# Score blocks of the dilated heads issued two query tiles at a time

## Chip, cores and metric

The kernel runs on one core of one Trainium2 chip. The metric is device time of one execution in microseconds (us). Where the text says TensorE, VectorE, ScalarE and GpSimd, the profile's rows say PE (PEld for its weight loads), DVE, ACT and POOL.

## What is computed

A two-layer encoder trunk on x of 1 x 1024 x 1024 (float32). Layer 0: RMS norm, one projection to queries, keys and values of 16 heads of width 64, of which eight are dilated sliding-window heads (mixer A) and eight 2-D neighbourhood heads; output projection, residual, SwiGLU feed-forward, residual. Layer 1: the same with eight differential heads. A last RMS norm. The change touches mixer A alone:

```
DILATED_PAIRS = ((128, 1), (512, 4), (2048, 16))

def dilated_window_branch(q, k, v, slopes, window, dilation):
    # query t attends to t + j*dilation, |j| <= window/(2*dilation)
    s = einsum(q, k) * HEAD_DIM ** -0.5 - slopes * dist
    s = where(valid, s, -inf)
    m = max(s); p = exp(s - m); l = sum(p)
    return einsum(p, v) / l, m + log(l)

def dilated_mixture_attention(q, k, v):
    # the three branches, weighted by softmax over their log denominators
```

## The kernel before

Everything is float32, and products are kept exact to float32 by splitting an operand into a high and a low part and adding two or three matmuls. Sizes: 1024 tokens are NQ = 8 query tiles of 128; two heads of a mixer make a head pair P. P = 0 to 3 are the dilated pairs (kind A), 4 to 7 the neighbourhood pairs (B), 8 to 15 the differential heads (C).

The order of every engine is written out by hand. `order(0)` runs through (P, n), head pair and query tile, and each engine has a loop body for that *turn*; engines meet at semaphores only. On TensorE (`attention_mixed`, line 2346) a turn of kind A holds:

- `qk(*after)`, line 2185: the scores of the **next** tile. For each head of the pair (m = 0, 1) three near matmuls (lines 2203 to 2209, 128 queries by 256 neighbouring keys) and three far ones (line 2213, queries and keys taken with a stride of four). They contract over 64 rows; the two heads lie on rows 0 to 63 and 64 to 127. Scores go to PSUM banks 2 (n % 2) + m, so tile n + 2 uses the banks of tile n, and `qk` waits until the exponentials of tile n have read them (`exp_done`). In turn 7 the block (tile 0 of the next pair) stands between the two transposes (`late_scores`).
- in even turns `pv`, lines 2274 and 2278: the product of the last two tiles' weights with the values, head 0 before `turn(.., 0)` and head 1 before `turn(.., 1)`.
- `turn`, line 2244: transposes of the exponentials of tile n, head 0 and head 1. They wait for `exp_done` and, since the transposed bank is used again, for the low part of the tile before (`lo_done`).
- `fill`, line 2147: matmuls of the projection for the next pair, in pieces given by the tables FILLS_AB (P < 3) and FILLS_TURN (P = 3). 24 of them make one 128 x 512 piece in the single fill bank 7; the first of a piece waits for `fill_evac`.
- `tv`, line 2160: transposes of the next pair's values, waiting for `vlo_done` and `fill_evac`; and in turn 1 of P = 1 to 5 `turn_stats`, lines 2169 and 2173, transposes of softmax statistics that wait for `y_done` and, from P = 2, for `al_done`.

VectorE in a turn: `evac` (lines 1491, 1493, 1496) of a finished fill piece, `ttr` (line 1525, bias and minimum of the next tile's scores, after `qk_done`), `y_add` (line 1613) of the output pieces, `lo` (line 1606, low part of the transposed exponentials), `vlo` (line 1509), `w_split` (line 1383). In turn 0 of P = 1 and 2 the evac stands near the turn's end, behind `y_add` (and from P = 2 behind `weights_last`, lines 1547 and 1551). In turn 4 of P < 3 the last `lo` is put off to turn 5 (`lower_later`), behind the evac. ScalarE: `y_copy` (line 994), `hi` (line 948), `exp` (line 913, two for each head, waiting for `ttr_done` and for the transposes of the tile before, because there is one exponential tile for each head), `kq_high` (line 928), `vhi` (line 941).

Of the kernel before, what the change touches and what calls it, by code (L numbers as in the profile page):

```python
# [25 lines left out]
NQ = T // 128  # L26
# [33 lines left out]
def key_tiles(kind, n):  # L60

    if kind != "B":
        return 0, NQ
    lo = max(0, min(2 * n - ROWS // 2, 2 * NQ - ROWS))
    hi = max(0, min(2 * n + 1 - ROWS // 2, 2 * NQ - ROWS)) + ROWS
    return lo // 2, (hi + 1) // 2 - lo // 2
# [14 lines left out]
def build(nc, x_in, wstrips, wdown, gains, subln, lams, ali_a, ali_c, tab_b, out):  # L81
# [141 lines left out]
    def kind_of(P):  # L223
        return "A" if P < 4 else "B" if P < 8 else "C"
# [162 lines left out]
    def fills_at(P, n):  # L387

        parts = FILLS_AB[n] if P < 3 else FILLS_TURN[n] if P == 3 else FILLS_B[n] if P < 8 else FILLS_LATE[n]
        if P == 2 and n == NQ - 1:  # L390
            return [parts[0], [(2, 2, 0, 8)]]
        if P == 8 and n == 0:
            return [[(0, 1, 7, 14)], [(0, 1, 14, 24)]]
        known = [(0, late(P)), (1, P % 8 < 7), (2, P < 2)]
        return [[p for p in part if (p[0], True) in known] for part in parts]
# [34 lines left out]
    def turned_v(P, n):  # L430

        if P == 0 and n < 2:
            return ([(0, 0), (0, 1)], [(0, 2), (0, 3)]) if n == 0 else ([(0, 4), (1, 0)], [(1, 1)])
        if 3 <= P < 8:
            return [(P, 1)] if late(P) and n == 1 else [], [(P + 1, 0)] if P < 7 and n == 7 else []
        if late(P):
            first, second = {0: ([], [0]), 1: ([1], [])}.get(n, ([], []))
            return [(P, b) for b in first], [(P, b) for b in second]
        first, second = {1: ([0], [1]), 3: ([2], [3]), 5: ([4], [])}.get(n, ([], []))
        return [(P + 1, b) for b in first], [(P + 1, b) for b in second]  # L440
# [20 lines left out]
    def order(layer):  # L461

        for g in range(8 * NQ):
            P, n = 8 * layer + g // NQ, g % NQ
            after = (8 * layer + (g + 1) // NQ, (g + 1) % NQ) if g + 1 < 8 * NQ else None
            last = (P, n - 1) if n else (P - 1, NQ - 1)
            yield P, n, after, last if g and n % 2 == 0 else None, P % 8 < 7
# [1596 lines left out]
    def pe_program(e):  # L2064
# [120 lines left out]
        def qk(P, n):  # L2185

            kind = kind_of(P)
            k0, nk = key_tiles(kind, n)
            if kind == "A":
                e.wait_ge(S["kq_lo"], 4 * P + (3 if n == 0 else 4))  # L2190
                if 8 * P + n > 1:
                    e.wait_ge(S["exp_done"], 1 + 2 * (8 * P + n - 1))
                if P == 0 and n == 0:
                    e.wait_ge(S["fill_evac"], 4)
                t = 128 * n - BAND
                near = slice(128 * n, 128 * n + 128)
                far = slice(n // 2 + 512 * (n % 2), 512 * (n % 2) + 512, NCLS)
                for i, (a, b) in enumerate(((0, 0), (0, 1), (1, 0))):
                    for m in range(2):
                        r = slice(64 * m, 64 * m + 64)  # L2200
                        ps, q, k = PS[:, 2 * (n % 2) + m, :], QS[r, a, near], KS[r, P % 2, b, :]
                        if 0 < n < NQ - 1:
                            e.matmul(ps[:, 0:256], q, k[:, t:t + 256], start=i == 0, stop=False)  # L2203
                        elif n == 0:
                            e.matmul(ps[:, 0:BAND], q, k[:, 0:BAND], start=i == 0, stop=False)
                            e.matmul(ps[:, BAND:256], q, k[:, 0:256 - BAND], start=False, stop=False)
                        else:
                            e.matmul(ps[:, 0:256 - BAND], q, k[:, t:T], start=i == 0, stop=False)
                            e.matmul(ps[:, 256 - BAND:256], q, k[:, T - BAND:T], start=False, stop=False)
                for i, (a, b) in enumerate(((0, 0), (0, 1), (1, 0))):  # L2210
                    for m in range(2):
                        r = slice(64 * m, 64 * m + 64)
                        last = e.matmul(PS[:, 2 * (n % 2) + m, 256:512], QS[r, a, far],  # L2213
                                        KS[r, P % 2, b, n // 2:T:NCLS], start=False, stop=i == 2)
                last.then_inc(S["qk_done"], 1)
                return
            e.wait_ge(S["kq_lo"], 4 * P + (3 if n < 4 else 4))
            e.wait_ge(S["exp_done"], 1 + 16 * P + 2 * n)
            if P == 8 and n == 0:
                e.wait_ge(S["fill_evac"], 6 * P + 3)  # L2220
            q = slice(128 * n, 128 * n + 128)
            for c in range(0, nk, 4):
                wd = 128 * min(4, nk - c)
                k = slice(128 * (k0 + c), 128 * (k0 + c) + wd)
                for i, (a, b) in enumerate(((0, 0), (0, 1), (1, 0))):
                    for m in range(2):
                        r = slice(64 * m, 64 * m + 64)
                        last = e.matmul(PS[:, S_BANK[m] + c // 4, 0:wd], QS[r, a, q], KS[r, P % 2, b, k],  # L2228
                                        start=i == 0, stop=i == 2)
            last.then_inc(S["qk_done"], 1)  # L2230
# [111 lines left out]
        def fills(parts, P, layer):  # L2342
            for ahead, k, a, b in parts:
                fill(P + ahead, k, a, b, layer)

        def attention_mixed():
            begin(0)
            for P, n, after, last, more in order(0):
                kind = kind_of(P)
                first_part, second_part = fills_at(P, n)  # L2350
                first, second = turned_v(P, n)
                late_scores = kind == "A" and n == NQ - 1
                late_turn = kind == "B" and n == NQ - 1 and P < 7
                if after and not late_scores:
                    qk(*after)
                if P == 0 and n == 1:
                    tv(*first.pop(0), P, n)
                if late_turn:
                    fills(first_part, P, 0)
                if last:  # L2360
                    if n == 2 and 1 <= P <= 5:
                        e.wait_ge(S["st_copy"], P)
                    if n == 4 and P >= 6:
                        e.wait_ge(S["rows_copied"], P - 5)
                    e.wait_ge(S["vlo_done"], issued(P, n))
                    pv(*last, 0)
                turn(P, n, 0, kind)
                if P == 0 and n == 0:
                    fill(1, 0, 0, 5, 0)
                    tv(0, 0, P, n)  # L2370
                    fill(1, 0, 5, 11, 0)
                    tv(0, 1, P, n)
                    turn(P, n, 1, kind)
                    fill(1, 0, 11, 16, 0)
                    tv(0, 2, P, n)
                    fill(1, 0, 16, 22, 0)
                    tv(0, 3, P, n)
                    fill(1, 0, 22, 24, 0)
                    continue
                if n == 1 and 1 <= P <= 5:  # L2380
                    turn_stats(P)
                if n == 3 and P >= 6:
                    turn_rows(P)
                if not late_turn:
                    fills(first_part, P, 0)
                if late_scores:
                    qk(*after)
                for v in first:
                    tv(*v, P, n)
                if last:  # L2390
                    pv(*last, 1)
                if not after:
                    op_item(0, 0)
                turn(P, n, 1, kind)
                if P < 3:
                    fills(BETWEEN_AB.get(n, []), P, 0)
                for v in second:
                    tv(*v, P, n)
                fills(second_part, P, 0)
            for m in range(2):  # L2400
                op_item(0, m + 1)
                pv(7, NQ - 1, m)
            op_item(0, 3)
            e.wait_ge(S["rwide_done"], 1)
            for n in range(NQ):
                last = e.matmul(PS[:, T_BANK + n // 4, 128 * (n % 4):128 * (n % 4) + 128],
                                BIAS0[:, 0, 128 * n:128 * n + 128], IDENT[:, :], start=True, stop=True)
            last.then_inc(S["lspread_done"], 1)
# [331 lines left out]
```

## Time and profile before

| | us |
|---|---|
| median of 3 runs | 2653.29 |
| lowest and highest | 2650.76, 2653.81 |
| the profiled execution, own time | 2651.4 |
| its span, first to last instruction | 2649.6 |
| mean granted clock of TensorE | 0.991 |
| first and last far score matmul of the dilated pairs, start | 45.4, 286.2 |

The profiled execution's time is its span and 1.8 us around it. Timeline rows give the start in us from the span's start, the time from start to end of a merged group, engine, line, operation and operands. Ends of matmuls are modelled and overlap the next one's start, so the text works with starts.

### The profile page before, as it was taken

The numbers are of one execution on the slowest core, as the hardware profiler recorded it, in microseconds if no ns is written. First come the engines' busy times: TensorE is split into PE (matmuls) and PEld (weight loads), VectorE is DVE, ScalarE is ACT, GpSimd is POOL, SyncE is SP. The second block draws the span as 40 slices with busy tenths as digits, with TensorE's granted clock in tenths as the row PEclk, the third lists the DMA queues.
The fourth block names the chain that finished last, engine by engine and source line by source line (L and its number), as shares of the span: only waits on it lengthen the run. The fifth ranks groups of instructions, "written<-read, shape, count | busy, mean of one in ns | idle before, by whom it ended". The sixth has DMA issues, their size and how long they took to land.

```text
span 2649.6 us, 37390 instructions
## 1 busy us (share of the span) xinstructions
PE 2616.7 (99%) x13531; PEld 2161.0 (82%) x13531; DVE 1774.7 (67%) x2918; ACT 1116.4 (42%) x1998; POOL 141.9 (5%) x142
## 2 busy tenths in 40 slices
PE   8999999899999999999999999999999999999998
PEld 6888878788888888888878888888888888888887
DVE  6566655655676666766777777777656677666766
ACT  5555645534323323333455555555343223323333
POOL 0001022400000000000000000000000000000001
PEclk9999999999999999999999999999999999999999
DMA  3123243521111111111311111111211111111112
GB/s 124 59 59 83 67 120 104 158 104 52 56 48 48 56 59 52 48 52 58 116 46 47 48 48 47 48 48 66 96 56 56 52 48 48 55 58 53 48 48 84
DMA packets 101725, 173.75 MB, mean 66 GB/s; under 512 B 27296, under 2 KB 36944, under 8 KB 100048
## 3 DMA queue, kind: packets, MB, share of 16 engines
q1 hardware_dynamic: 90560, 162.26, 19.4%
q10 hardware_dynamic: 11024, 9.60, 1.3%
q8 instruction: 90, 1.47, 0.2%
q14 instruction: 51, 0.42, 0.0%
HBM read 151.74 MB, written 20.08 MB: 65 GB/s over the span
## 4 chain that ended last, share of the span: by engine, by line
PE 93%; DVE 2%; ACT 2%; issue 1%; SPq 1%; DMA 1%; POOL 0%; ACTq 0%; POOLq 0%; DVEq 0%
PE PS L2147 19%; PE PS L2067 18%; PE PS L2069 18%; PE PS L2068 18%; PE PS L2228 5%; PE PS L2297 5%; PE PS L2253 4%; PE PS L2244 1%; PE PS L2213 1%; PE PS L2274 1%; PE PS L2160 1%; PE PS L2278 1%; SPq L516 0%; PE PS L2203 0%; PE PS L2074 0%
## 5 line engine op out<-in xcount | busy, mean ns | idle before, releaser
L2147 PE MATMUL PS<-HH,WS 128*128 128x512 f32 x1536 | 518.1, 404 | 9.3 <-DVE HL L1405 8.1
L1182 ACT ACTIVATE WS<-WR 128x512 fp32r<-128x512 f32 x254 | 159.3, 629 | 432.3 <-PE PS L2069 310.3
L2147 PEld LDWEIGHTS PS<-HH,WS 128*128 128x128 f32 x1536 | 286.6, 189 | 66.8 <-DVE WS L1411 7.2
L2147 PE MATMUL PS<-HL,WS 128*128 128x512 f32 x768 | 302.8, 394 | 0.0
L2067 PE MATMUL PS<-AH,WS 128*128 128x512 f32 x704 | 275.5, 391 | 0.0
L2069 PE MATMUL PS<-AH,WS 128*128 128x512 f32 x704 | 274.7, 390 | 0.0
L2068 PE MATMUL PS<-AL,WS 128*128 128x512 f32 x704 | 274.6, 390 | 0.0
L1863 DVE TENSOR_TENSOR X<-PS,X 128x512 f32<-128x512 f32 x352 | 231.2, 686 | 63.1 <-PE PS L2069 62.9
L2067 PE MATMUL PS<-TH,WS 128*128 128x512 f32 x640 | 249.0, 389 | 0.0
L2068 PE MATMUL PS<-TL,WS 128*128 128x512 f32 x640 | 249.0, 389 | 0.0
L2069 PE MATMUL PS<-TH,WS 128*128 128x512 f32 x640 | 249.0, 389 | 0.0
L1805 DVE TENSOR_TENSOR WS<-WR,WS 128x512 fp32r<-128x512 f32 x254 | 174.9, 689 | 108.5 <-ACT WS L1182 105.0
L2067 PE MATMUL PS<-FH,WS 128*128 128x512 f32 x608 | 237.2, 390 | 0.5 <-DVE SIL L1857 0.5
L2069 PE MATMUL PS<-FH,WS 128*128 128x512 f32 x608 | 236.6, 389 | 0.0
L2068 PE MATMUL PS<-FL,WS 128*128 128x512 f32 x608 | 236.5, 389 | 0.0
L1531 DVE CUSTOM_DVE_ANT_0 PS<-PS,BIASC 128x1024 f32<-128x1024 f32 x128 | 154.3, 1247 | 26.3 <-PE PS L2228 25.2
L2147 PEld LDWEIGHTS PS<-HL,WS 128*128 128x128 f32 x768 | 145.8, 190 | 25.8
L2069 PEld LDWEIGHTS PS<-AH,WS 128*128 128x128 f32 x704 | 132.5, 188 | 27.7
L2067 PEld LDWEIGHTS PS<-AH,WS 128*128 128x128 f32 x704 | 132.6, 188 | 27.2
L2068 PEld LDWEIGHTS PS<-AL,WS 128*128 128x128 f32 x704 | 132.5, 188 | 27.3
L2228 PE MATMUL PS<-KS,QS 64*128 64x512 f32 (+1 forms) x1056 | 145.7, 406 | 1.5 <-ACT EC L918 0.9
L918 ACT ACTIVATE EC<-PS,ST 128x1024 f32<-128x1024 f32 x128 | 141.2, 1114 | 3.5 <-DVE ST L1531 3.5
(251 smaller groups left out, 4575.8 us busy)
## 6 DMA issues: line engine op xcount, KB each, us to landing
WR<-wstrips SPq DMA_DIRECT2D x304, 256.0 KB, 2.7
DR<-wdown SPq DMA_DIRECT2D x88, 256.0 KB, 2.6
BIASC<-ali_c SPq DMA_DIRECT2D x8, 960.0 KB, 6.9
BIAS<-tab_b SPq DMA_DIRECT2D x4, 1536.0 KB, 9.8
Y<-y_scratch SPq DMA_DIRECT2D x12, 512.0 KB, 8.1
BIAS<-ali_a SPq DMA_DIRECT2D x4, 1152.0 KB, 8.0
ya_scratch<-YS ACTq DMA_DIRECT2D x32, 128.0 KB, 2.4
MA<-a_scratch SPq DMA_DIRECT2D x16, 256.0 KB, 4.8
```

The lines of the kernel that those rows point to most:

```text
L918: e.activation(e_tile(kind, m, n, P)[:, 0:128 * nk], banks(S_BANK[m], 2)[:, 0:128 * nk], ACT.Exp, scale=-1.0, bias=ST[:, n % 2, m:m + 1], ...
L1182: e.activation(WS[:, slot, 0, :], src, ACT.Copy).then_inc(S["w_hi"], 1)
L1531: e.tensor_tensor_reduce(out=s, in0=s, in1=(table if kind == "C" else table[:, m, :])[:, c:c + 128 * nk], scale=-1.0 if kind == "B" else 1 ...
L1805: e.tensor_tensor(WS[:, slot, 1, :], src, f(WS[:, slot, 0, :]), ALU.subtract).then_inc(S["w_lo"], 1)
L1863: e.tensor_tensor(xs, PS[:, D_BANK + at % 4, :], xs, ALU.add).then_inc(S["d_free"], 1)
L2067: e.matmul(ps, wh, xh, start=start, stop=False, skip_group_check=on)
L2068: e.matmul(ps, wh, xl, start=False, stop=False, skip_group_check=on)
L2069: return e.matmul(ps, wl, xh, start=False, stop=stop, skip_group_check=on)
L2147: last = e.matmul(ps, wt, xt, start=g == 0, stop=g == 23)
L2228: last = e.matmul(PS[:, S_BANK[m] + c // 4, 0:wd], QS[r, a, q], KS[r, P % 2, b, k], start=i == 0, stop=i == 2)
L2253: last = e.transpose(PS[:, bank + k // 4, 128 * (k % 4):128 * (k % 4) + 128], src[:, 128 * k:128 * k + 128], IDENT[:, :])
L2297: last = e.matmul(PS[:, bank, lo_:hi_], v, p, start=i == 0, stop=i == len(todo) - 1)
```

## The change

Kind A alone is touched. In turns 0, 2 and 4 of a pair TensorE issues two score blocks, those of tiles n + 1 and n + 2, in turn 6 one (tile 7), and in turns 1, 3 and 5 none. Turn 7 is as before. The other engines' programs are the same, instruction for instruction.

```diff
@@ -2351,7 +2351,10 @@
                 first, second = turned_v(P, n)
                 late_scores = kind == "A" and n == NQ - 1
                 late_turn = kind == "B" and n == NQ - 1 and P < 7
-                if after and not late_scores:
+                if kind == "A" and not late_scores:
+                    for ahead in range(n + 1, min(n + 3, NQ)) if n % 2 == 0 else []:
+                        qk(P, ahead)
+                elif after and not late_scores:
                     qk(*after)
                 if P == 0 and n == 1:
                     tv(*first.pop(0), P, n)
```

TensorE at the head of turn 0 of P = 1: what stands there in the changed kernel against before (lines 2203 and 2213 are a score block, 2274 the start of PV).

```order
 L2203 MATMUL PS<-KS,QS 128x256 x5
 L2213 MATMUL PS<-KS,QS 128x256 x6
+L2203 MATMUL PS<-KS,QS 128x256 [waits exp_done,kq_lo]
+L2203 MATMUL PS<-KS,QS 128x256 x5
+L2213 MATMUL PS<-KS,QS 128x256 x6
 L2274 MATMUL PS<-ATA,VS 128x256 [waits y_done,lo_done,vlo_done]
 L2274 MATMUL PS<-ATA,VS 128x256
```

The scores of tile 2 now stand directly behind those of tile 1, ahead of PV and of everything else in the turn.

TensorE from the end of turn 0 to the first fills of turn 1 of P = 1, before (line 2147 is a fill, 2244 the transposes of exponentials, 2169 the transpose of statistics):

```order
L2147 MATMUL PS<-HH,WS 128x512
L2203 MATMUL PS<-KS,QS 128x256 [waits exp_done,kq_lo]
L2203 MATMUL PS<-KS,QS 128x256 x5
L2213 MATMUL PS<-KS,QS 128x256 x6
L2244 MATMUL PS<-IDENT,E_75 128x128 [waits lo_done,exp_done]
L2244 MATMUL PS<-IDENT,E_75 128x128 x3
L2169 MATMUL PS<-IDENT,SM 32x128 [waits vlo_done,y_done,exp_done]
L2147 MATMUL PS<-HH,WS 128x512 [waits fill_evac]
```

and in the changed kernel:

```order
L2147 MATMUL PS<-HH,WS 128x512
L2244 MATMUL PS<-IDENT,E_75 128x128 [waits lo_done,exp_done]
L2244 MATMUL PS<-IDENT,E_75 128x128 x3
L2169 MATMUL PS<-IDENT,SM 32x128 [waits vlo_done,y_done,exp_done]
L2147 MATMUL PS<-HH,WS 128x512 [waits fill_evac]
```

Between the last fill of turn 0 and the fill that waits for `fill_evac`, the twelve score matmuls are gone.

## Rows read from the trace of the kernel before

**Rows 1.** The page's parts 1 and 2: busy times, and TensorE's granted clock.
```profile
PE 2616.7 (99%) x13531; PEld 2161.0 (82%) x13531; DVE 1774.7 (67%) x2918; ACT 1116.4 (42%) x1998; POOL 141.9 (5%) x142
...
PEclk9999999999999999999999999999999999999999
```

**Rows 2.** The page's part 4, chain that ended last, by engine.
```profile
PE 93%; DVE 2%; ACT 2%; issue 1%; SPq 1%; DMA 1%; POOL 0%; ACTq 0%; POOLq 0%; DVEq 0%
```

**Rows 3.** Timeline, PE, P=1, turns 2 and 3 (several narrow windows): start, length, instruction.
```profile
141.15 0.60 PE L2244 MATMUL PS<-IDENT,E 128*128 128x128 f32 x4
141.50 0.47 PE L2147 MATMUL PS<-HL,WS 128*128 128x512 f32 x1
...
142.97 0.40 PE L2147 MATMUL PS<-HL,WS 128*128 128x512 f32 x1
...
143.64 0.28 PE L2203 MATMUL PS<-KS,QS 64*128 64x256 f32 x2
143.75 0.73 PE L2213 MATMUL PS<-KS,QS 64*128 64x256 f32 x4
...
144.07 0.65 PE L2213 MATMUL PS<-KS,QS 64*128 64x256 f32 x4
...
144.30 0.42 PE L2213 MATMUL PS<-KS,QS 64*128 64x256 f32 x2
...
145.06 0.48 PE L2147 MATMUL PS<-HH,WS 128*128 128x512 f32 x1
```

**Rows 4.** Timeline, P=1, end of turn 0 and turn 1: ACT, DVE, PE.
```profile
125.03 0.47 ACT L913 ACTIVATE E<-PS,SM 128x256 f32<-128x256 f32 x1 [1.58 <-PE PS L2244]
...
126.07 0.59 ACT L994 ACTIVATE YS<-PS 64x512 f32<-64x512 f32 x1
...
127.44 0.67 DVE L1493 TENSOR_TENSOR FS<-PS,RSTD 128x512 f32<-128x512 f32 x1
...
128.35 0.48 PE L2147 MATMUL PS<-HH,WS 128*128 128x512 f32 x1
```

**Rows 5.** Timeline, P=1, turn 5: DVE, PE.
```profile
160.29 0.67 DVE L1493 TENSOR_TENSOR FS<-PS,RSTD 128x512 f32<-128x512 f32 x1
...
161.22 0.48 PE L2147 MATMUL PS<-HH,WS 128*128 128x512 f32 x1
```

**Rows 6.** Timeline, P=1, turn 3: DVE, PE.
```profile
146.26 0.69 DVE L1606 TENSOR_TENSOR ATA<-PS,ATA 128x512 fp32r<-128x512 f32 x1
147.64 0.69 DVE L1493 TENSOR_TENSOR FS<-PS,RSTD 128x512 f32<-128x512 f32 x1 [0.70 <-PE PS L2147]
...
148.39 0.50 PE L2147 MATMUL PS<-HH,WS 128*128 128x512 f32 x1
```

**Rows 7.** Timeline, P=0, turn 1: DVE, PE.
```profile
61.07 0.69 DVE L1509 TENSOR_TENSOR VC<-PS,VC 128x512 fp32r<-128x512 f32 x1 [1.53 <-ACT VC L941]
...
62.15 0.33 PE L2160 MATMUL PS<-IDENT,FS 128*128 128x128 f32 x1
```

**Rows 8.** Timeline, P=3, turns 1, 2 and 4: DVE, ACT, PE.
```profile
256.27 0.19 DVE L1551 TENSOR_TENSOR CA<-CE,CW 128x32 f32<-128x32 f32 x1
...
256.52 0.28 PE L2173 MATMUL PS<-IDENT,CA 128*32 128x128 f32 x1
...
259.49 0.96 PE L2213 MATMUL PS<-KS,QS 64*128 64x256 f32 x6
...
260.29 0.21 ACT L913 ACTIVATION_READ_ACCUMULATOR E<-PS,SM 128x1 f32 x1
...
273.59 0.21 ACT L913 ACTIVATION_READ_ACCUMULATOR E<-PS,SM 128x1 f32 x1
...
273.24 0.87 PE L2274 MATMUL PS<-ATA,VS 128*128 128x256 f32 x6
...
276.75 0.39 PE L2147 MATMUL PS<-HH,WS 128*128 128x512 f32 x1
277.24 0.47 PE L2274 MATMUL PS<-ATA,VS 128*128 128x256 f32 x2
```

## The prediction, made before the changed kernel was run

> **What bounds the kernel now.** I read the busy shares first. TensorE (PE) is busy for 99% of the span, the granted clock is the upper level of 2.4 GHz (a 9 in every slice of its row), and VectorE and ScalarE have a third and more to spare [rows 1]. The chain that ended last is PE for 93% of its length [rows 2]. So the time is the length of PE's own queue plus the places where that queue stands still, and a change that only reorders PE must be judged on two things: how much shorter the queue becomes, and which results are no longer ready when PE comes for them. The third view is the timeline of single PE instructions around a score block, and the fourth the timelines of ScalarE (ACT) and VectorE (DVE) over the same microseconds.
>
> A *turn* is one pass of the loop, one query tile n of one head pair P. A *score block* is one call of qk: six near and six far matmuls on 64 rows.
>
> **What a score block costs alone, and behind another.** Around the block at the head of turn 3 of P=1 [rows 3], the last fill matmul starts at 142.97 and the first fill behind the block and the transposes at 145.06, 2.09 us. Without a block it would be one fill (six of them run from 141.50 to 142.97, 0.24 each) and four transposes (141.15 to 141.50, 0.35), 0.59. The block therefore costs 2.09 - 0.59 = 1.50 us. Inside it the pace is quicker: the last near pair takes 143.75 - 143.64 = 0.11, the first far pair 0.32, the second 0.23. A block with another 64-row block on both sides would be 3 x 0.11 + 0.32 + 2 x 0.23 = 1.11 to 1.13; I take 1.13. The other 0.37 is paid at the change from 128-row to 64-row matmuls and back. The trace has no two blocks in a row, so the saving of a pairing is bounded from above by that 0.37 and from below by nothing at all (the switch could be paid again at the semaphore wait between the two); I take 0.37, because inside a block near and far matmuls follow each other with no such pause. With 12 pairings (tiles 1+2, 3+4, 5+6 of four head pairs) PE's queue becomes 12 x 0.37 = 4.4 us shorter.
> The Trainium skill (TensorEngine Tiling (Array Packing), Key Properties) states that changing the tiling mode drains TensorE while moving between tiles of one mode doesn't; by that rule alone the change would be worth those 4.4 us, and the trace agrees as far as the 0.37 above goes. The same page of the Trainium skill (PSUM Bottleneck) warns that tiling quickens TensorE but not the emptying of PSUM; it gives no price, and speaks the other way.
>
> **What the moved block was covering.** At an odd turn the block stood between the last fills of the even turn and the first work of the odd one. Remove it and PE arrives 1.50 us earlier, relative to everything that ACT and DVE still have to finish from the even turn. Those chains start from PE instructions (last transposes, last PV) that are themselves 1.13 us later, since the extra block stands ahead of them. So a pairing costs 1.13 minus the smaller of 1.50 and the slack at the first wait of the odd turn. With slack above 1.50 it would be -0.37; with no slack it is +1.13. I take the slack from the rows, with 0.06 us from the end of a DVE instruction to the start of the waiting matmul (147.64 + 0.69 = 148.33 to 148.39 in [rows 6]).
>
> *Turn 1, P=1* [rows 4]. Behind the even turn's last transposes ACT runs two exponentials (from 125.03), the copy for the output (126.07), DVE the addition and then evac, whose last instruction ends at 127.44 + 0.67 = 128.11; only then may the fill start that re-uses the fill bank. It starts at 128.35, could at 128.17: slack 0.18, cost 1.13 - 0.18 = +0.95. P=2 is taken as the same; there DVE has two more small instructions in front of that evac, so it is between 0.95 and 1.13.
> *Turn 5, P=1* [rows 5]. The evac that frees the fill bank ends at 160.29 + 0.67 = 160.96; the fill starts at 161.22. Slack 0.20, cost +0.93, three times (P=0, 1, 2).
> *Turn 3, P=1* [rows 6]. Here the evac waits for fills that PE itself brings forward, but DVE has to finish a low part at 146.26 + 0.69 = 146.95 first, so evac ends at 147.64 and the fill can start at 147.70 instead of 148.39. Slack 0.69, cost +0.44, three times.
> *Turn 1, P=0* [rows 7]. PE's first work is the transpose of V that waits for DVE's low part, ended at 61.07 + 0.69 = 61.76. It starts at 62.15, could at 61.82. Slack 0.33, cost +0.80.
> That is 0.80 + 2 x 0.95 + 3 x 0.93 + 3 x 0.44 = 6.8 us for P=0 to 2.
>
> *P=3* has fewer fills per turn and is tighter [rows 8]. Turn 1: the transposes of statistics wait for a DVE result that ends at 256.27 + 0.19 = 256.46 and start at 256.52: slack nil, +1.13. Turn 2: the second block (tile 4) overwrites the banks of tile 2 and must wait for its exponentials, which end at 260.29 + 0.21 = 260.50; PE would be there at 259.49 + 0.78 = 260.27. So 0.29 of waiting and the 1.13, +1.42. What turn 3 would give back, turn 4 takes: its second block (tile 6) waits for the exponentials of tile 4, ended at 273.59 + 0.21 = 273.80 behind DVE's own queue. From 273.86 the block takes 1.13, so the first PV starts at 274.99, not 273.24: +1.75, of which the wait in front of the second PV (276.75 + 0.23 to 277.24, 0.26) takes 0.26 back: +1.49. (The way back to 128 rows, up to 0.1, is left out.) Turns 5 and 6 run behind ACT and DVE and give nothing. P=3 costs 1.13 + 1.42 + 1.49 = 4.0 us.
>
> **Sum.** 6.8 + 4.0 = +10.8 us against the profiled execution's own 2651.4, that is 2662.2. The median of the runs shown lies 1.9 above that execution (2653.3), so the forecast is 2664.1. DVE, ACT and the DMA queues issue the same instructions in the same order; in odd turns DVE finds its scores ready earlier, which costs nothing and gains only where DVE waits for scores and someone waits for DVE. Nothing behind turn 7 of P=3 changes but by the shift. About 0.2% (5.3 us) is what a measurement here can tell from no change.
>
> **Rivals.**
> *The odd turns keep their cover (faster).* If ACT and DVE end the even turn's chains at least 1.5 us sooner, because the early scores empty their queues, every pairing is worth -0.37: 2653.3 - 4.4 = 2648.9. This is what the mode-switch rule of the Trainium skill (TensorEngine Tiling (Array Packing), Key Properties) would give with nothing else in play. It decides where the slack is above 1.13, the point at which a pairing turns from loss to gain. Against it: the chain of turn 1 starts at the even turn's last transposes and has no idle time for scores in it [rows 4].
> *The second block drains too.* If the wait between the two blocks costs the pause again, each pairing loses 0.37 more: 10.8 + 4.4 = +15.2, 2668.5. For it: no two blocks stand together in the trace. Against it: the smooth pace inside a block [rows 3].
> *Half the loss.* In turns 3 and 5 and in P=3 a DVE queue stands ahead of the result; if scores that are there early pull half of it forward, some +5.4 remain, 2658.7.
> *No change that can be measured*: the losses meet waits that exist already. The only ones seen are parts of a microsecond in P=3.
>
> **How the numbers follow.** Forecast 0.70, second drain 0.10, half the loss 0.10, gain 0.04, no change 0.06. Half the loss lies on the border, so it is shared: faster 0.04, the same 0.10, slower 0.86. The forecast itself may be off by 0.1 us at each of twelve waits and by 2 us in P=3, which gives 2660 to 2668; taking in most of the two neighbours the range is 2657.5 to 2669.5.
>
> **What would show it.** In the changed profile: the second block's first near pair follows the last far pair by some 0.23 us; the idle time of PE in front of the fills at odd turns 1 and 5 (released by evac, line 1493) grows to over 1 us each and to 0.8 us in turn 3; a wait for exponentials appears in front of the second blocks of P=3; the stretch from the first to the last turn of the four dilated pairs is 10 to 12 us longer and everything behind it as long as before. A stretch that is shorter, or odd turns without idle time, would show the slack argument wrong.

## The result, and the profile after

| | before | changed |
|---|---|---|
| median of 6 runs, us | 2651.32 | 2665.32 |
| lowest and highest | 2647.81, 2653.81 | 2664.05, 2666.84 |
| the profiled execution, own time | 2651.4 | 2664.05 |
| its span | 2649.6 | 2662.3 |

The ratio is 1.0053, with a 95% interval of 1.0043 to 1.0064: slower by 14.0 us in the medians, by 12.7 us in the two profiled executions. The forecast was 2664.1 and slower, on a median of before of 2653.3; with six runs that median is 2.0 us lower.

The page of the changed kernel, parts 1 and 4:

```profile
PE 2616.6 (98%) x13531; PEld 2162.6 (81%) x13531; DVE 1777.7 (67%) x2918; ACT 1116.2 (42%) x1998; POOL 141.8 (5%) x142
...
PE 90%; DVE 4%; ACT 2%; issue 1%; SPq 1%; DMA 1%; ACTq 0%; POOL 0%; POOLq 0%; DVEq 0%
```

PE is busy for the same 2616.6 us as before (2616.7, [rows 1]); what has grown is the time in which it stands still, and the chain that ended last runs three points less over PE and two more over DVE [rows 2]. Who ends PE's idle time in the dilated stretch, from the view of waits of the changed kernel (engine, instruction, who ended it: us in total, times, longest):

```profile
PEld PS L2147 <- DVE FS L1493: 8.4, 9, 1.3
...
PE PS L2147 <- DVE FS L1493: 6.4, 9, 1.1
...
PE PS L2169 <- issue: 2.7, 3, 1.7
...
PE PS L2203 <- ACT E L913: 1.6, 2, 1.4
PE PS L2244 <- DVE ATA L1606: 1.4, 2, 0.7
PE PS L2160 <- DVE VC L1509: 1.0, 1, 1.0
```

and in the same stretch of the kernel before:

```profile
PEld PS L2147 <- DVE FS L1493: 0.8, 1, 0.8
...
PE PS L2147 <- DVE FS L1493: 0.6, 1, 0.6
```

Nine fills now wait for an evacuation where one did. These are turns 1, 3 and 5 of P = 0 to 2; the one in turn 1 of P=0 was there before. Line 2169, the transpose of statistics in turn 1 of P = 1 to 3, waits too: the view names no releaser, but in P=1 it starts at 130.23, 0.10 behind the end of VectorE's addition (the first row of DVE below), whose semaphore it waits for. The timeline of PE at the first two kinds of place that the prediction spoke of, the pair of blocks in turn 0 of P=1 (a row from a narrow window first) and the start of turn 1:

```profile
121.09 0.42 PE L2213 MATMUL PS<-KS,QS 64*128 64x256 f32 x2
121.33 0.54 PE L2203 MATMUL PS<-KS,QS 64*128 64x256 f32 x6
121.70 0.97 PE L2213 MATMUL PS<-KS,QS 64*128 64x256 f32 x6
...
129.13 0.60 PE L2244 MATMUL PS<-IDENT,E 128*128 128x128 f32 x4
130.23 0.27 PE L2169 MATMUL PS<-IDENT,SM 128*32 128x128 f32 x1 [0.50 <-issue]
130.91 0.50 PE L2147 MATMUL PS<-HH,WS 128*128 128x512 f32 x1 [0.41 <-DVE FS L1493]
```

and DVE over the same time:

```profile
129.45 0.68 DVE L1613 TENSOR_TENSOR YS<-PS,YS 64x512 f32<-64x512 f32 x1 [3.44 <-ACT YS L994]
130.06 0.20 DVE L1491 TENSOR_TENSOR FS<-PS,RSTD 128x64 f32<-128x64 f32 x1
130.19 0.67 DVE L1493 TENSOR_TENSOR FS<-PS,RSTD 128x512 f32<-128x512 f32 x1
```

The second block follows the first after 0.24 us, the pace of far pairs, and its near part takes 0.37 instead of 0.45. Then, 9 us later, the evacuation ends at 130.86 and the fill starts at 130.91, 0.05 behind it. In [rows 4] the fill was 0.24 behind. The transposes at 129.13 were early and the fill had to wait all the same.

**Where the 12.7 us are.** I compare the starts of the transposes of head 1 in both traces, turn by turn, both counted from the first score block. The difference grows by 1.15 in every even turn of P = 0 to 2 that has a pair, and the odd turns give part of it back. (In turn 3 the fill that waits stands behind these transposes. They come 1.5 us sooner, and the wait takes 0.7 of it back before turn 4; the table counts it with turns 2 and 3.)

| pairing | forecast | measured |
|---|---|---|
| P=0, turns 0 and 1 | +0.80 | 1.15 - 0.26 = +0.89 |
| P=1, turns 0 and 1 | +0.95 | 1.15 - 0.16 = +0.99 |
| P=2, turns 0 and 1 | +0.95 | 1.15 - 0.01 = +1.14 |
| P=0 to 2, turns 2 and 3, each | +0.44 | +0.33 |
| P=0 to 2, turns 4 and 5, each | +0.93 | +0.98 |
| sum, P=0 to 2 | +6.8 | +7.0 |
| P=3, turns 0 and 1 | +1.13 | +1.13 |
| P=3, the rest | +2.9 | +5.0 |
| dilated stretch | +10.8 | +13.1 |

The other 0.4 us lie outside the stretch, where both kernels issue the same: the changed trace reaches its first score block 0.6 us sooner, and behind the stretch the difference wanders between 10.9 and 14.3 us and ends at 13.3. TensorE's clock falls there in both kernels, not in the same places: its mean is 0.87 from 510 to 550 us in the trace before and 0.91 from 523.4 to 563.4 in the changed one. A second trace of the changed kernel (below) has the same 13.1 in the stretch and ends at 10.9, so what lies outside the stretch differs by 2 us between executions.

**P=3.** The excess lies in turn 4. PE of the changed kernel there:

```profile
280.67 0.96 PE L2213 MATMUL PS<-KS,QS 64*128 64x256 f32 x6
283.06 0.62 PE L2203 MATMUL PS<-KS,QS 64*128 64x256 f32 x6 [1.42 <-ACT E L913]
283.49 0.99 PE L2213 MATMUL PS<-KS,QS 64*128 64x256 f32 x6
284.40 1.15 PE L2274 MATMUL PS<-ATA,VS 128*128 128x256 f32 x6
285.35 1.16 PE L2278 MATMUL PS<-ATA,VC 128*128 128x256 f32 x4
286.31 1.06 PE L2244 MATMUL PS<-IDENT,E 128*128 128x128 f32 x4
```

The wait for the exponentials of tile 4 is the one forecast. But PV, up to the transposes behind it, takes 1.91 us from 284.40 to 286.31, where before it took 1.24, from 273.24 [rows 8] to this row:

```profile
274.48 0.60 PE L2244 MATMUL PS<-IDENT,E 128*128 128x128 f32 x4
```

The view of windows (stretch, its length, busy us of each engine, granted clock, DMA share, GB/s) tells why:

```profile
281.00:284.40 3.40, 1.98 (x18) 1.49 (x16) 2.82 (x10) 2.92 (x10) 0.41 (x1) 1.00 0.40 142
284.40:288.50 4.10, 4.10 (x20) 3.86 (x19) 2.41 (x10) 1.69 (x5) 0.87 (x1) 0.58 0.00 0
288.50:292.00 3.50, 3.50 (x24) 3.13 (x23) 0.22 (x1) 0.78 (x3) 0.00 (x0) 1.00 0.00 0
```

The granted clock was 1.00 up to 284.4, 0.58 on average in the next 4.1 us, so for most of them the lower level of 1.2 GHz, and 1.00 again. In the 3.4 us ahead of it PE had been busy for 1.98.

### The profile page after: what moved, and what is told of

Same layout as the page of the kernel before. It is cut to its first block, busy times and chain, and to the rows that moved or that the text cites. A ratio compares the mean times of both kernels' runs of the same rounds, so it can differ in the third digit from the quotient of the medians.

```text
span 2662.3 us, 37390 instructions
## 1 busy us (share of the span) xinstructions
PE 2616.6 (98%) x13531; PEld 2162.6 (81%) x13531; DVE 1777.7 (67%) x2918; ACT 1116.2 (42%) x1998; POOL 141.8 (5%) x142
## 4 chain that ended last, share of the span: by engine, by line
PE 90%; DVE 4%; ACT 2%; issue 1%; SPq 1%; DMA 1%; ACTq 0%; POOL 0%; POOLq 0%; DVEq 0%
PE PS L2147 18%; PE PS L2067 18%; PE PS L2068 18%; PE PS L2069 18%; PE PS L2228 5%; PE PS L2297 4%; PE PS L2253 3%; PE PS L2213 1%; PE PS L2274 1%; PE PS L2244 1%; PE PS L2160 1%; PE PS L2278 1%; PE PS L2074 1%; SPq L516 1%; ACT E L913 0%
```

## The experiments

Positions are read as above: the shift of the transposes of head 1 against the kernel before, from the first score block on. "To P=3" is that shift at the end of turn 7 of P=2, "P=3" what its turns add. The pairing as changed gives +7.0 and +6.1.

**Pairings in P = 0 to 2 alone.**

```diff
-                if kind == "A" and not late_scores:
+                if kind == "A" and P < 3 and not late_scores:
```

> The pairing is done for head pairs P = 0 to 2 alone. Theory (each moved block had covered a chain on ScalarE and VectorE; a pairing costs 1.15 us of insertion less the slack at the odd turn): the dilated stretch grows by the 7.0 us that the changed kernel shows up to the first turn of P = 3, so +7 us, near 2658, and the granted clock stays at its upper level in the whole dilated stretch. Rival (the loss comes from the second block's wait for exponentials, which only P = 3 has): within 1 us of before or faster by 9 x 0.37 = 3.3 us.

Measured: ratio 1.0025 (1.0015 to 1.0036), 2658.7 against 2651.4, +7.3. To P=3 the shift is 8.3, of which 1.3 come at once in turn 1 of P=0. The clock had fallen there, against the expectation:

```profile
63.00:70.00 7.00, 5.52 (x23) 4.41 (x24) 3.84 (x13) 2.32 (x8) 0.00 (x0) 0.76 0.00 0
```

All other turns of P = 0 to 2 repeat the changed kernel's steps to 0.04 us, and P=3 adds 0.0. The rival falls: the nine pairings without any wait for exponentials lose by themselves.

**Pairings in P = 3 alone.**

```diff
-                if kind == "A" and not late_scores:
+                if P == 3 and not late_scores:
```

> The pairing is done for P = 3 alone. Theory: +6.1 us, the share that the changed kernel shows between the first turn of P = 3 and its end: 1.1 at turns 0 and 1, 5.0 at turns 2 to 6. Of the 5.0 some 1.7 is the half clock of 3.4 us behind the wait in turn 4, which should come again, since the wait is the same 1.4 us long. If the half clock needs the idle time gathered over P = 0 to 2, it is missing here and the growth is 4.4. Rival (pairing saves the mode switch and P = 3 is not special): -1.1 us.

Measured: 1.0023 (1.0013 to 1.0034), +5.9 in the medians. The shift in P=3 of the profiled execution is +4.5: 1.15, 1.62 and 1.74 for the three pairings. The granted clock is 1.00 over the whole stretch, behind the same wait in turn 4:

```profile
44.00:305.00 261.00, 254.76 (x1626) 210.41 (x1625) 153.38 (x437) 149.19 (x419) 22.81 (x26) 1.00 0.23 61
```

PE there, with the wait:

```profile
276.98 0.62 PE L2203 MATMUL PS<-KS,QS 64*128 64x256 f32 x6 [1.42 <-ACT E L913]
277.42 0.99 PE L2213 MATMUL PS<-KS,QS 64*128 64x256 f32 x6
278.33 0.90 PE L2274 MATMUL PS<-ATA,VS 128*128 128x256 f32 x6
```

So the changed kernel's 6.1 are 4.5 of insertion and waits and 1.6 of half clock, and in this execution the wait in turn 4 alone didn't bring the half clock. It is one execution, and the fastest of the eight (2655.19; the others are 2655.8 to 2661.7). The median's +5.9 is near the 6.1 that was expected with the fall, so the executions that were not profiled may well have had one; no trace shows them.

**The two blocks apart in the same turn.** The second block stands behind the transposes of head 0.

```diff
                 turn(P, n, 0, kind)
+                if kind == "A" and n in (0, 2, 4):
+                    qk(P, n + 2)
```

with `qk(P, n + 1)` alone at the head of even turns.

> As the changed kernel, but in turns 0, 2 and 4 the second score block stands behind the transposes of head 0 instead of directly behind the first block. Theory: the blocks no longer share a mode switch, so each of the nine even turns of P = 0 to 2 grows by 1.50 instead of 1.15, while the odd turns wait as before: +3.2 us over the changed kernel up to the first turn of P = 3. In P = 3 the wait for exponentials shrinks, because PE has work in front of it. If two adjacent blocks save nothing, the stretch up to P = 3 is the same as in the changed kernel.

Measured: 1.0051 (1.0036 to 1.0066). Each even turn of P = 0 to 2 grows by 1.55 instead of 1.15, the odd turns give back what they did, and to P=3 the shift is +10.7, 3.7 more than in the changed kernel. The second block alone, in turn 0 of P=1:

```profile
124.55 0.60 PE L2244 MATMUL PS<-IDENT,E 128*128 128x128 f32 x4
125.08 0.62 PE L2203 MATMUL PS<-KS,QS 64*128 64x256 f32 x6
...
126.43 0.50 PE L2147 MATMUL PS<-HL,WS 128*128 128x512 f32 x1
```

From the transposes to the first fill behind them it is 1.88 us, without a block 0.35 (141.15 to 141.50 in [rows 3]): alone the block costs some 1.5 us, behind another 1.15. That is the saving of a shared mode switch: by the shifts 0.40 us a pairing, forecast 0.37. P=3 adds only 4.3, with no wait for exponentials and a clock of 1.00 throughout, so in the traces the whole stretch is 1.9 us longer than the changed kernel's. The medians are alike (2665.4 and 2665.3); no run shows what makes up for these 1.9 us.

**The evacuation ahead of the addition.** Changed kernel, VectorE's turn 4 of P < 3 (and the evacuation taken out of turn 5):

```diff
+                if n == 4 and P < 3:
+                    evac(P + 1, 3)
                 if last:
                     y_add(*last, 1)
```

> As the changed kernel, but VectorE does the evacuation of the key piece that opens turn 5 of P = 0 to 2 (piece 3 of the next pair) ahead of the last output addition of turn 4, instead of behind it. Theory: the fill at the head of turn 5 waits for exactly that evacuation, behind the addition; without the addition in front it comes 0.6 us sooner, in each of three turns: the wait there falls from 1.3 to about 0.7 us, 1.8 us in all, and the first turn of P = 3 comes 1.8 us earlier than in the changed kernel. Rival (the wait ends with something else, such as transposes or ScalarE): no change.

Measured: 1.0041 (1.0025 to 1.0056), 2661.5, and 2.1 us less shift to P=3 than in the changed kernel: 0.70, 0.71 and 0.74 in turn 5 of P = 0, 1 and 2, nothing anywhere else. Turn 5 of P=1, DVE and PE (PE's lines are two higher here):

```profile
164.07 0.69 DVE L1493 TENSOR_TENSOR FS<-PS,RSTD 128x512 f32<-128x512 f32 x1 [3.32 <-PE PS L2149]
164.68 0.67 DVE L1613 TENSOR_TENSOR YS<-PS,YS 64x512 f32<-64x512 f32 x1
```

```profile
163.88 0.60 PE L2246 MATMUL PS<-IDENT,E 128*128 128x128 f32 x4
164.82 0.50 PE L2149 MATMUL PS<-HH,WS 128*128 128x512 f32 x1 [0.35 <-DVE FS L1493]
```

In the changed kernel the transposes were at 163.42, the evacuation at 164.35 to 165.02 and the fill at 165.08, with 1.05 us of idle time. The two traces have shifted against each other by then, so count from the transposes: the fill starts 0.94 us behind them here and 1.66 there. The wait ends with this evacuation and with nothing else.

**The same move in the kernel before.**

> The kernel before, with the evacuation that opens turn 5 of P = 0 to 2 moved ahead of the last output addition of turn 4. Theory: there the score block covers the chain and 0.2 us of slack are left, so the 0.7 us that the same move gave in the changed kernel are worth nothing: the first turn of P = 3 comes within 0.1 us of before. Rival (a sooner evacuation always helps): 2 us earlier.

Measured: 0.9998 (0.9988 to 1.0007); shift to P=3 0.0. What is worth 2.1 us in the one kernel is worth nothing in the other: there the score block still covers the chain.

**Work put into the hole.** Changed kernel, in turn 1 of P = 1 and 2 and turn 5 of P = 0 to 2, ahead of the transposes of head 0 and behind the waits that these have:

```diff
+                if (n == 1 and P in (1, 2)) or (n == 5 and P < 3):
+                    e.wait_ge(S["exp_done"], 1 + 16 * P + 2 * n + 1)
+                    e.wait_ge(S["lo_done"], 1 + t_count(P, n, 0, kind) - 2)
+                    for again in range(3):
+                        for i, k in enumerate((2, 0, 3, 1)):
+                            e.transpose(PS[:, T_BANK, 128 * i:128 * i + 128],
+                                        e_tile(kind, 0, n)[:, 128 * k:128 * k + 128], IDENT[:, :])
```

> As the changed kernel, but in turn 1 of P = 1 and 2 and turn 5 of P = 0 to 2 TensorE repeats the four transposes of head 0 three times before it does them (the same values into the same place), some 1.1 us of work in each of five places, 5.3 us in all, where the score block stood before. Theory: PE has 1.3 us of idle time there, in which that work disappears; the fill that waits for the evacuation starts when it did, and the first turn of P = 3 comes as in the changed kernel, within 0.3 us. Rival (PE's queue is what counts, there is no chain with a fixed end): 5.3 us later.

Measured: 1.0048 (1.0033 to 1.0064), 2665.3. The shift to P=3 is the changed kernel's to 0.02 us, though each place has 1.3 us more of PE work, some 6.5 us in all. Turn 1 of P=1:

```profile
130.63 1.47 PE L2375 MATMUL PS<-IDENT,E 128*128 128x128 f32 x12
131.94 0.60 PE L2244 MATMUL PS<-IDENT,E 128*128 128x128 f32 x4
132.37 0.27 PE L2169 MATMUL PS<-IDENT,SM 128*32 128x128 f32 x1
132.41 0.50 PE L2147 MATMUL PS<-HH,WS 128*128 128x512 f32 x1
```

DVE's evacuation ends at 131.68 + 0.67 = 132.35. The fill starts 0.06 behind it, as without the extra work. The removed score block had been free of charge at these places for the same reason, but for the 0.2 us of slack. (In P=3 this run has 1.0 us more, with a granted clock of 0.72 from 264 to 270; from 284 to 290 it is 0.74, the fall in turn 4 that the changed kernel has too.) The waits in turn 3 and in turn 1 of P=0 were not tested in this way; for them there are the traces alone.

**Pairs in odd turns.** Turn 0 forms tile 1, turns 1, 3 and 5 form two tiles, turns 2, 4 and 6 none.

```diff
-                    for ahead in range(n + 1, min(n + 3, NQ)) if n % 2 == 0 else []:
+                    for ahead in [1] if n == 0 else [n + 1, n + 2] if n % 2 else []:
```

> The pairing turned round: turn 0 forms tile 1 alone, turns 1, 3 and 5 form tiles 2 and 3, 4 and 5, 6 and 7, turns 2, 4 and 6 none. The same count of mode switches is saved. Theory (1.15 less the slack at the next turn): from the timeline of before for P = 1, turn 2 has 1.30 us of slack at the fill behind its evacuation, turn 4 has 0.3 at the first PV (values' low part ended 152.44, PV at 152.82), turn 6 has more than the block's 1.6: net -0.15, +0.85 and -0.37 to -0.45, so about +0.3 for a pair and +1 up to the first turn of P = 3; P = 3 itself between 0 and +4. In all 2652 to 2656, well under the changed kernel. Rival (any moved block costs about a microsecond): as the changed kernel.

Measured: 1.0018 (1.0009 to 1.0027), 2657.3, clock 1.00 throughout the stretch. It is better than the changed kernel by 8 us and worse than before, as expected in direction, but the size was off: +4.7 to P=3 instead of +1. The pairing at turns 3 and 4 cost 0.97 (expected 0.85), but the one at turns 1 and 2 cost 0.39 (expected -0.15) and the one at 5 and 6 0.26 (expected about -0.4). I had looked at the first wait of each turn. A second one stands further in: the second PV of turn 2 waits for the addition that frees its bank, which VectorE does behind the next tile's scores. PE and DVE of P=1, turn 2:

```profile
141.98 0.68 DVE L1613 TENSOR_TENSOR YS<-PS,YS 64x512 f32<-64x512 f32 x1
...
142.81 0.65 PE L2274 MATMUL PS<-ATA,VS 128*128 128x256 f32 x4 [0.28 <-DVE YS L1613]
```

Turn 6 has the same wait (0.29 of idle time in P=1). Turn 5 also grows by 1.49 instead of 1.15, since its second block is tile 7, at the edge, whose near part is twelve matmuls (lines 2208 and 2209) instead of six. P=3 adds 1.5 us, inside the 0 to 4 that were expected.

**Without the last pairing of P = 3.** As the changed kernel, with tile 6 formed in turn 5.

> As the changed kernel, but in P = 3 tiles 5 and 6 are formed apart, as before: tile 5 in turn 4, tile 6 in turn 5. Theory: the wait of 1.4 us for the exponentials of tile 4 and the half clock behind it are gone; P = 3 costs 1.15 for the first pairing and about 1.6 less the 0.6 of turn 3 for the second, some 2.2 us instead of 6.1, near 2661. If the half clock hangs on the stall in turn 4 it doesn't come in the dilated stretch.

Measured: 1.0036 (1.0023 to 1.0049). P=3 adds 3.8: 1.2, then 2.7 in turn 2, -0.6 in turn 3 and +0.6 in turn 4. The wait and the half clock of turn 4 are gone, but the clock is 0.76 from 264 to 271, in turn 2, and its step is 1.0 above the 1.6 of other runs. Without that it would be 2.8, of which the 0.6 in turn 4 was not expected: what turn 3 gives back, turn 4 loses again. PE is idle for 0.72 us in front of the first PV there, until 285.86, and VectorE's low part, which that PV needs, ends at 285.76 behind the scores of tile 5.

**The changed kernel twice more.**

> The changed kernel once more, for its trace. The score blocks, waits and the +7.0 us up to the first turn of P = 3 should come to within 0.1 us, as they do in every kernel so far. Open is TensorE's half clock in the dilated stretch: it came at 284.9 us in the changed kernel, at 65.4 with P = 0 to 2 alone, at 266 or 267 in two others and not at all in three. If it belongs to the 1.4 us wait of turn 4 of P = 3, it comes at 284.9 again; if only the start of a fixed rhythm against the idle time decides, it comes elsewhere or not at all, and P = 3 costs 4.5 us where it doesn't.

> The same once more, for the same question: where in the dilated stretch, if at all, the clock falls to half, and what P = 3 costs then: 6.1 us with it in turn 4, 4.5 without.

Measured: 2662.6 and 2667.8 us, one execution each, on another chip, where one of the kernel before took 2653.0. Both have the fall in turn 4 of P=3 and +6.1 there; the second has another in turn 1 of P=0, 1.3 us, which makes its shift to P=3 8.3 instead of 7.0. (The list of falls in the expectation left out two in turn 4 of P=3, those of the runs with the evacuation moved, clock 0.72 from 281 to 287, and with extra work.)

```profile
64.00:71.00 7.00, 5.39 (x21) 3.87 (x21) 3.84 (x13) 2.38 (x7) 0.00 (x0) 0.76 0.00 0
286.00:293.00 7.00, 5.59 (x31) 5.12 (x32) 4.69 (x15) 4.06 (x13) 1.27 (x1) 0.76 0.09 36
```

## Why the prediction was right, and where it was short

*The saving.* Forecast 12 x 0.37, measured 0.40 a pairing by setting the blocks apart. The pause at a change between 128 and 64 rows is real and is not paid again at the semaphore wait between two blocks, which was the upper rival: in P = 0 to 2, where that wait is over when PE comes to it, the second block follows after 0.24 us. The rule of the Trainium skill that changing the tiling mode drains TensorE (TensorEngine Tiling (Array Packing), Key Properties) agrees with these 0.40 us; taken alone it would have given the sign wrong.

*The cover.* That a block inserted ahead of the chains costs 1.13 and an odd turn gives back only its slack is what the nine pairings of P = 0 to 2 show, +7.0 for +6.8. The sum is closer than its terms, which were off by -0.1 to +0.2 each and partly cancel. The signs named ahead came in part: in front of the fill PE is idle for 1.05 us in turn 5 and 0.6 in turn 3, but in turn 1 of P=1 for 0.41, because 0.50 of the wait already falls in front of the transposes of statistics. Three runs show the mechanism and not only the sum: the evacuation moved forward gives 2.1 us in the changed kernel and none in the one before, and extra work in the hole costs nothing. The slack of P=2, turn 1, which I took from P=1, was nil, the upper of the two bounds given. Turn 3 gave back all of 1.5 at its last transposes and lost it again, but for 0.8, at the fill behind them; 0.7 was the slack read there.

*P=3.* The first pairing came as worked out. The other two were forecast at 1.42 + 1.49 = 2.9 and are 1.62 + 1.74 = 3.4 in the run with P=3 alone. The term was mis-sized because I let the waiting block start at full pace and put 1.13 us from its start to the first PV; it takes 1.34 (283.06 to 284.40). From standstill its near part takes 0.43 instead of 0.37, and the way back to 128 rows, which I had left out, is paid too. The places are right: PE waits for the exponentials of tiles 2 and 4.

*What was missing.* The half clock, 1.6 us in turn 4 of P=3. No term of the sum allowed for it. It is the larger part of the difference between +10.8 and +13.1. The remaining 0.9 of the 14.0 between the medians is less than the 2 us by which two traces of the changed kernel differ outside the stretch.

*The number.* 2664.1 against 2665.3 is in part luck. The growth was forecast at 10.8 us and is 14.0 between the medians, 3.2 too little; the median of before that it was added to, of three runs, was 2.0 too high, and the two errors cancel for the most part.

*The rivals.* The gain and the second drain are refuted by the trace and by the run with the blocks apart. "Half the loss" would have needed early scores to pull VectorE's chains forward; the waiting fill came 0.1 us sooner than the slack allowed in turn 3 and in no other turn of P = 0 to 2, and the stretch lost 13.1, not 5.4. "No change" falls with the 14.0 us.

## What to carry to other kernels

A block of PE work that depends on nothing recent is cover. Before it is moved, ask what stands behind it in the queue and when that becomes ready: a move costs its length in the new place, less what the old place gives back, and that is the slack there, at most the block's length. The slack is read between the end of the releasing instruction and the start of the waiting one, for every waiting instruction of the turn and not the first alone. Saving a mode switch of 0.4 us pays only where that slack is above what is inserted, 1.15 us here. None of the places tried had that: the best, turn 6 in the run with pairs in odd turns, gave back 1.23, but there the inserted block was an edge tile's and cost 1.49.

## What the hardware did that was not expected

TensorE's granted clock fell to its lower level inside a stretch in which it had stayed at 1.00 before. In all three traces of the changed kernel, in the one with the evacuation moved and in the one with extra work it fell in turn 4 of P=3, behind a wait of 1.4 us, and cost 1.5 to 1.6 us. In the one trace of the run with P=3 alone the same wait brought no fall. Other kernels of the study had a fall in turn 2 of P=3 (1.0 us, two runs) or in turn 1 of P=0 (1.3 us, two runs, one of them a repeat of the changed kernel, whose other two traces have none there). Each of these falls stands behind a wait of PE: 1.4 us in turn 4, 1.65 in turn 1 of P=3, 1.05 and 0.5 in turn 1 of P=0. The same waits stand in other traces without a fall behind them, and the kernel before has falls too, behind the dilated stretch (a mean clock of 0.87 from 510 to 550 us). What decides between two places alike, or two executions of the same kernel, is open: no run varied the idle time alone. For the reckoning it means that a wait on PE may cost more than its length: here a wait of 1.4 us was followed, in five traces of six, by slow work that cost another 1.5 to 1.6. That the wait is the cause is not shown.
